# Two attention heads in one transpose of the output, and three pieces of work moved by up to one unit

## The reference

```python
z = jnp.einsum("bsd,dc->bsc", rms_norm(x, norm_mix_g), w_in)      # columns B | C | h | q | k | v, 512 each
y_conv = B * (conv3(C * h) + conv_b)                              # causal, width 3, by channel
q, k = rms_norm(q, q_gain), rms_norm(k, k_gain)                   # 8 heads of 64
scores = jnp.einsum("bnqhd,bnkhd->bhnqk", q, k_band) * 64 ** -0.5 + bias   # chunks of 64, this and 8 before
o = jnp.einsum("bnhqk,bnkhd->bnqhd", softmax(scores), v_band)
x = x + concat(group_rms_norm(y_conv), group_rms_norm(o)) @ w_out # groups of 64
out = x + square(relu(rms_norm(x, norm_mlp_g) @ w_mlp_in)) @ w_mlp_out
```

## Time and profile before

| | us |
|---|---|
| median of 3 runs | 1124.91 |
| lowest, highest | 1124.46, 1125.86 |
| the profiled execution | 1123.81 |
| its span, first to last instruction | 1122.0 |
| PE busy in it | 1100.3 |
| DVE, ACT, POOL busy in it | 714.0, 538.9, 629.2 |

### The profile page before, as it was taken

The page is one execution under the profiler, slowest core; times in us unless marked ns, Lnnn a source line. Parts: engine busy times, 40 slices in busy tenths (PEclk is TensorE's granted clock), DMA queues, the critical chain, the costliest instruction groups (busy, mean ns, idle before and its releaser), DMA issues.

```text
span 1122.0 us, 14684 instructions
## 1 busy us (share of the span) xinstructions
PE 1100.3 (98%) x5272; PEld 918.0 (82%) x5272; DVE 714.0 (64%) x899; ACT 538.9 (48%) x885; POOL 629.2 (56%) x368
## 2 busy tenths in 40 slices
PE   5999999999999999999999999999999999999998
PEld 5888888888888878887888888888878888888887
DVE  6677757767766785335435353534477767777798
ACT  6664665465476563225454545445453243333330
POOL 4322141230412030267778888787789697796992
PEclk9999999999999999999999999999999999999999
DMA  8311110120110514121464444444687435345324
GB/s 254 107 38 38 41 56 16 40 58 19 56 29 31 188 58 150 57 75 62 155 197 151 153 150 149 150 146 163 236 287 244 155 122 188 129 134 204 113 76 168
DMA packets 98511, 135.79 MB, mean 121 GB/s; under 512 B 8072, under 2 KB 52112, under 8 KB 98456
## 3 DMA queue, kind: packets, MB, share of 16 engines
q1 hardware_dynamic: 95104, 131.13, 34.9%
q10 hardware_dynamic: 3352, 3.94, 1.2%
HBM read 97.27 MB, written 39.34 MB: 122 GB/s over the span
## 4 chain that ended last, share of the span: by engine, by line
PE 93%; POOL 2%; DVE 2%; DMA 1%; ACT 1%; issue 1%; ACTq 0%; SPq 0%; POOLq 0%; DVEq 0%
PE PJ L1530 22%; PE PJ L1785 10%; PE SC L1785 9%; PE OS L1785 7%; PE PJ L1608 7%; PE PJ L1822 7%; PE SC L1822 7%; PE PT L1822 6%; PE OS L1822 6%; PE OS L1590 3%; PE PT L1577 2%; PE SC L1567 1%; PE SC L1566 1%; PE SC L1608 1%; DMA b<-in_w_mlp_out 1%
## 5 line engine op out<-in xcount | busy, mean ns | idle before, releaser
L1530 PE MATMUL PJ<-actT,wsl 128*128 128x512 f32 (+1 forms) x1176 | 298.2, 396 | 1.0 <-DVE actT L1012 0.9
L1530 PEld LDWEIGHTS PJ<-actT,wsl 128*128 128x128 f32 x1176 | 209.7, 190 | 38.9 <-DVE actT L1012 1.7
L614 POOL TENSOR_TENSOR ring<-b,ring 128x1024 fp32r<-128x1024 f32 x48 | 139.0, 2905 | 34.9 <-ACT ring L957 34.6
L1434 DVE TENSOR_TENSOR ring<-hraw,ring 128x1024 fp32r<-128x1024 f32 x56 | 148.8, 2693 | 3.5 <-ACT ring L952 3.5
L505 POOL CAST wsl<-raw 128x1024 fp32r<-128x1024 f32 x24 | 26.0, 1082 | 197.3 <-PE PJ L1530 164.5
L952 ACT ACTIVATE ring<-hraw 128x1024 fp32r<-128x1024 f32 x56 | 59.2, 1057 | 131.3 <-PE OS L1822 60.1
L1785 PE MATMUL OS<-actT,w1a 128*128 128x512 f32 x384 | 93.6, 391 | 0.8 <-ACT p1s L893 0.8
L731 ACT ACTIVATE prob<-prob,negm 128x640 f32<-128x640 f32 (+4 forms) x64 | 44.4, 694 | 90.8 <-DVE negm L1117 90.6
L1785 PEld LDWEIGHTS OS<-actT,w1a 128*128 128x128 f32 x384 | 71.6, 188 | 15.6 <-issue 1.2
L1822 PE MATMUL PJ<-ring 128*128 128x512 f32 x336 | 80.6, 390 | 2.1 <-POOL ring L614 2.1
L1822 PE MATMUL PT<-ring 128*128 128x512 f32 x336 | 80.8, 390 | 0.1
(11 more groups left out here) (195 smaller groups left out, 2189.0 us busy)
## 6 DMA issues: line engine op xcount, KB each, us to landing
hraw<-hidd SPq DMA_DIRECT2D x56, 512.0 KB, 3.7
w1r<-in_w_mlp_in SPq DMA_DIRECT2D x16, 1024.0 KB, 6.3
hidd<-hs SPq DMA_DIRECT2D x64, 256.0 KB, 2.0
b<-in_w_mlp_out SPq DMA_DIRECT2D x16, 1024.0 KB, 7.0
raw<-in_w_in SPq DMA_DIRECT2D x24, 512.0 KB, 3.8
hidd<-h SPq DMA_DIRECT2D x48, 256.0 KB, 2.3
xin<-in_x SPq DMA_DIRECT2D x8, 512.0 KB, 8.6
woraw<-in_w_out SPq DMA_DIRECT2D x8, 512.0 KB, 9.0
```

What stands on the lines that cost most here:

```text
L614: nc.gpsimd.tensor_tensor(duo(n)[1][LO], W2_SRC[name][:, 2 * d:2 * d + 2], duo(n)[1][HI].bitcast(F32), ALU.subtract).then_inc(s["wl2_done" ...
L1434: vec.tensor_tensor(duo(n)[0][LO], hraw[:, n % HRING], duo(n)[0][HI].bitcast(F32), ALU.subtract).then_inc(s["hl2_done"], 1)
L1530: last = mm(PJ[:, g % 2, cols], wsl[:, w % NSLOT, a, k], actT[:, b, k, c], start=(r == 0), stop=(r == 3 * KD - 1))
```

## The change

**Two heads in one transpose.** `u_sum` now makes two instructions. A reduce on the lower 64 partitions of UP adds the two halves of columns there (V's HI), into the half of `uT` that belongs to the unit's head. Then an add takes UP's upper 64 partitions (V's LO), of which only the columns of `pT` HI are read, onto it; the product LO*LO, which was summed before, falls away. It waits for the reduce by a new semaphore, `fold_done`. So `uT` holds two heads, 64 partitions each, and `pair_transpose` runs once for two units, in the heads of the odd units from 3 on and once behind unit 15. `o_sum` becomes a copy of 128 columns. `prob_v(u)` waits for `us_done` of the unit before, as no transpose ahead of it does so any longer.

**Moves.** DVE: V's remainder `v_lo(it, 1)` from 7a to 6b, `inverse(4, 0)` from 11a to 11b. PE: `sum_squares(4)` from 10b to 11a; `sum_squares(it+1, 1)` behind 22 projections from the last `prob_v` on, and not 18; the number of projections of the turn stays 54. ACT: `deviation(4)` from unit 10 to unit 11. In the last pass `pair_transpose(7)` stands behind `sum_squares(5)` and six products of `w_out`, as `u_transpose(15)` did. No DMA is changed.

The diff:

```diff
--- before.py
+++ after.py
@@ -212,7 +212,7 @@
         p1s_done r11_done u2_done u4_done c12_done c21_done c22_done
         rl11_done rl12_done rl21_done rl22_done h11_done h12_done h21_done h22_done hs_done
         b11_in b12_in b21_in b22_in hh2_done wh2_done hl2_done wl2_done ts_done d2_done dr_done
-        acc_in acc_zero fin_done
+        acc_in fold_done fin_done
         """.split()
         s = {n: ctx.enter_context(nc.semaphore(n)) for n in names}
         PRIMED = 3
@@ -795,6 +795,7 @@
                     if u == 10:
                         o_dev(it, 0)
                         c_copy(it, 1)
+                    if u == 11:
                         deviation(it, 4)
                     if u == 12:
                         o_store(it, 0)
@@ -1127,18 +1128,19 @@
             def u_sum(it, u):
 
                 dve.wait_ge(s["pv_done"], it * UNITS + (u + 1))
-                if u >= 2:
-                    dve.wait_ge(s["uq_done"], it * UNITS + (u - 1))
-                vec.tensor_reduce(uT[:, u % 2], UP.rearrange("p b c -> p c b"), AX.X, ALU.add
-                                  ).then_inc(s["us_done"], 1)
+                j, rows = u // 2, HEADS[u % 2]
+                if j >= 2 and u % 2 == 0:
+                    dve.wait_ge(s["uq_done"], it * (UNITS // 2) + j - 1)
+                vec.tensor_reduce(uT[rows, j % 2], UP[0:HD].rearrange("p b c -> p c b"), AX.X, ALU.add).then_inc(s["fold_done"], 1)
+                dve.wait_ge(s["fold_done"], it * UNITS + (u + 1))
+                vec.tensor_tensor(uT[rows, j % 2], UP[HD:P, 0], uT[rows, j % 2], ALU.add).then_inc(s["us_done"], 1)
 
             og = on[:, :, :].rearrange("p g (u d) -> p g u d", d=HD)
 
             def o_sum(it, j):
 
-                dve.wait_ge(s["uq_done"], it * UNITS + 2 * (j + 1))
-                vec.tensor_reduce(og[:, j // 4, 2 * (j % 4):2 * (j % 4) + 2], UQ.rearrange("p (u a d) -> p u d a", u=2, a=2),
-                                  AX.X, ALU.add).then_inc(s["oq_done"], 1)
+                dve.wait_ge(s["uq_done"], it * (UNITS // 2) + j + 1)
+                vec.tensor_copy(on[:, j // 4, j % 4 * P:(j % 4 + 1) * P], UQ[:, j % 2 * P:(j % 2 + 1) * P]).then_inc(s["oq_done"], 1)
 
             def per_unit(a):
                 return a[:, :].rearrange("p (u o) -> p u o", o=1).broadcast_to([P, 8, HD])
@@ -1198,8 +1200,9 @@
                     qk_lo(it, 2)
                 if at == "6a":
                     qk_lo(it, 3)
+                if at == "6b":
+                    v_lo(it, 1)
                 if at == "7a":
-                    v_lo(it, 1)
                     conv_gate(it, 0)
                 if at == "7b":
                     conv_tap(it, 0, 0)
@@ -1214,6 +1217,7 @@
                     squares_lo(it, 4)
                 if at == "11a":
                     o_norm(it, 0)
+                if at == "11b":
                     inverse(it, 4, 0)
                 if at == "12a":
                     inverse(it, 4, 1)
@@ -1584,6 +1588,8 @@
                 pe.wait_ge(s["ptlo_done"], it * UNITS + (u + 1))
                 if u == 0:
                     pe.wait_ge(s["vlo_done"], it * 2 + 1)
+                if u:
+                    pe.wait_ge(s["us_done"], it * UNITS + u)
                 if u % 2 == 0 and u:
                     pe.wait_ge(s["oq_done"], it * (UNITS // 2) + u // 2)
                 for j in range(nb):
@@ -1592,9 +1598,9 @@
                               start=(j == 0), stop=(j == nb - 1))
                 last.then_inc(s["pv_done"], 1)
 
-            def u_transpose(it, u):
-                pe.wait_ge(s["us_done"], it * UNITS + (u + 1))
-                nc.tensor.transpose(UQ[:, u % 2 * P:(u % 2 + 1) * P], uT[:, u % 2], ident[:, :]).then_inc(s["uq_done"], 1)
+            def pair_transpose(it, j):
+                pe.wait_ge(s["us_done"], it * UNITS + 2 * (j + 1))
+                nc.tensor.transpose(UQ[:, j % 2 * P:(j % 2 + 1) * P], uT[:, j % 2], ident[:, :]).then_inc(s["uq_done"], 1)
 
             def o_transpose(it, g, turn):
                 pe.wait_ge(s["on_done"], it * 2 + (g + 1))
@@ -1645,7 +1651,7 @@
                         sum_squares(it, 3)
                     if at == "4b":
                         v_transpose(it, 1)
-                    if at == "10b":
+                    if at == "11a":
                         sum_squares(it, 4)
                     if at == "12a":
                         o_transpose(it, 0, OTURN[0])
@@ -1664,8 +1670,8 @@
                 fill(4)
                 for u in range(UNITS):
                     count = (FILL_LAST if last else FILL)[u] - (4 if u == 0 else 0)
-                    if u >= 2:
-                        u_transpose(it, u - 2)
+                    if u >= 3 and u % 2:
+                        pair_transpose(it, u // 2 - 1)
                     if u + 1 < UNITS:
                         score(it, u + 1)
                     fill(count // 2)
@@ -1679,23 +1685,21 @@
 
                     rest = REST + 4 * 3 * KD - n
                     fill(rest - 54)
-                    u_transpose(it, UNITS - 2)
                     prob_v(it, UNITS - 1)
                     fill(8)
-                    u_transpose(it, UNITS - 1)
-                    fill(10)
+                    pair_transpose(it, UNITS // 2 - 1)
+                    fill(14)
                     sum_squares(it + 1, 1)
-                    fill(18)
+                    fill(14)
                     v_transpose(it + 1, 0)
                     fill(18)
                     o_transpose(it, 1, OTURN[1])
                 else:
                     assert n == REST
-                    u_transpose(it, UNITS - 2)
                     prob_v(it, UNITS - 1)
                     sum_squares(it, 5)
                     w_out_both(1, (1,))
-                    u_transpose(it, UNITS - 1)
+                    pair_transpose(it, UNITS // 2 - 1)
                     for k in range(2, KD):
                         w_out_both(k)
                         if k == 4:
```

## The result

The changed kernel takes 1130.11 us (median of 10 runs, 1127.19 to 1132.35), beside 1125.22 for the kernel before on the same chip (10 runs, 1124.25 to 1126.52). The ratio is 1.0046, 95% interval 1.0038 to 1.0055: slower by 4.9 us, where 2.6 us less was predicted. The profiled execution took 1129.81 us, its span 1128.0 (before 1122.0).

What follows compares the result with a forecast made beforehand. PE, busy 98% of the span, was taken as the bound. Passes 0 to 2 gave -2.39, the turns -0.6, the last pass +0.35: -2.6 us off 1124.91, so 1122.3 us, range 1120.2 to 1126.0.

Steps and rivals of the forecast that it cites:

- The wait for `sql` at the turn: Between passes, PE's 0.59 us wait for POOL goes or falls under 0.1; about 0.2 net gained, -0.6 over three turns.
- The first minimum: At the turn, PE's score(1) must wait for unit 0's minimum from DVE; 0.15 to 0.24 of the 0.59 stays.
- The two instructions of the fold: u_sum on DVE becomes a reduce of 0.42 and an add of 0.29; the next instruction starts 0.43 later.
- The two taps of unit 13: Passes 0 to 2: DVE taps alternate with POOL, end where they did; one of 8 transposes gives nothing, leaving -0.80 per pass.
- the last pass is late at `pT` and at `ym_lo(0)`: Last pass: PE waits longer for unit 13's pT and gets ym_lo(0) about 1.0 us later.
- Rival A: At the turn POOL takes the port first, kL's second subtract waits, 1.1 later three times: 1125.6 us; chance 0.25.
- Rival C: The add across halves costs twice the nearest row or more, u_sum +0.9; several units wait: 1128.8 us; chance 0.10.
- the transposes: On PE in the four passes, 32 fewer at 0.114 us each: -3.65 us if PE stays the limit.
- step 1: In unit 6, the pT remainder's 1.13 us spare shrinks to 0.16, the closest of the ordinary units, still without a wait.
- step 2: Last pass: ym_lo(0) about 1.0 us later, against five transposes and the tail's: +0.35 us instead of -0.91.

Runs made afterwards that it cites:

- e4: Changed kernel with q's remainder of the second half, qk_lo(2), made on DVE behind unit 4 instead of unit 5: 1127.07 us, ratio 1.0016.
- e1: Kernel before with the fold and pair transposes alone, all moves undone: 1133.02 us, ratio 1.0073.
- e2: Kernel before with the moves alone, one transpose a head as before: 1124.82 us, ratio 1.0005.
- e3: Changed kernel with sum of squares 4 and its root back at their old places in the last pass only: 1129.66 us, ratio 1.0032.
- e8: Kernel before with two unread DVE products added ahead of unit 13's taps in the last pass: 1128.66 us, ratio 1.0029.
- e6: Changed kernel with the score of unit 15 computed three times instead of once in the last pass: 1128.60 us, ratio 1.0020.
- e12: e11 with o_sum(6) ahead of ym_lo(1) on DVE in the last pass: 1122.60 us, ratio 0.9982.
- e7: e5 with the repeated score of e6 added: 1124.92 us, ratio 0.9992.
- e10: Kernel before with one unread DVE product added at 13a in the last pass: 1125.36 us, ratio 1.0010.
- e5: Changed kernel with the edits of e3 and e4 together: 1125.43 us, ratio 0.9997.
- e11: e5 with a tap at 12b outside the last pass, ym_lo(0), o_sum(6) and pair transpose 6 reordered in it, and e6's repeated score: 1124.19 us, ratio 0.9993.

## Why the prediction was wrong

**Right.** The wait for `sql` at the turn went: from `prob_v(15)` to V's transpose it is 9.6 us for 10.1, where 0.59 was forecast. The first minimum took a part back, as forecast: PE is 0.16, 0.07 and 0.32 later behind `score(1)` of passes 1 to 3, for 0.15 to 0.24. The two instructions of the fold cost 0.42 + 0.29. The two taps of unit 13 still end where POOL lets them, and `prob_v(13)` waits 0.25 instead of 0.15, so the one transpose fewer ahead of it gives nothing; the last pass is late at `pT` and at `ym_lo(0)`. Rival A did not happen: the second `kL` row in the turn stayed at its length. Rival C did not either, as the add costs no more than its nearest row; that its 1128.8 is near the result is luck. Passes without the new wait (e4: 93.8) are 0.6 shorter than before's, where the forecast had 1.0; 0.17 of the difference is e4's own new wait at `prob_v(4)`. No run left out the transposes alone; pass 0 of the changed kernel prices them at 0.13 to 0.14 each.

**Wrong, step 1: "That is the closest of the ordinary units; 0.16 remain."** I asked for each unit when its `pT` remainder was ready, and not for the other things that a score waits for. `score(8)` also reads `kL` of the half of k made just before, and had about 0.2 to spare with two sums ahead of it. e1 has the wait with the fold alone, e2 has none without the fold, and e4 takes it away. A pass was to take 93.45 us and took 94.49 in the mean. For the sum: the span grew by 6.0 us, of which 4.0 are half clock, so 2.0 is left where -2.6 was forecast. Of the 4.6 between them, 3.2 arose in passes 0 to 2 (+0.17 for -3.0), which is three of these waits at 1.1 each. In the last pass the products of `w_out` start 2.16 later, where the forecast's term gave 0.43 (1.0 less five transposes): 1.7 more, of which 1.0 is the fourth wait and 0.5 stands under step 2. The changed kernel's pass 0 begins 0.3 earlier, ahead of anything that was changed.

**Wrong, step 2: the last pass as "+0.35", at full clock.** The lateness in this term was too small: from `score(15)` to the products of `w_out` it is 5.90 us (396.94 to 402.84), before 4.43 (396.38 to 400.81), so 1.47 more, where I had 1.0. e3, with the root at its old place, has 0.96 more, so the moved root has 0.5 of it, for which I had 0.26. Its price was wrong altogether: I took every duration of PE from a profile at 1.00 and did not ask whether longer pauses would change that. In the profile after, pauses of 1.8 + 0.7 + 0.8 us stand in 5.4 us (397.4 to 402.8; before 0.8 + 0.3 + 0.8). Behind the second the clock falls to half for 6.8 us, and 2.4 us are lost by the rows; 1.6 more go in the second stretch. e8 makes the loss without the change, e6 makes it rarer by adding work, and in e12's profile it is gone.

The Trainium skill, "TensorE: Matmul & The Clock Gate", Part 1 (The HAM clock gate), says that the gate goes back to half rate when PE has been idle, and warns of an idle gap longer than any pause in front of a first stretch here. On the two levels the trace agrees (six products in 1.66 or in 2.93 us). On the gap it does not: the longest of those pauses was 2.0 us (e8), and in e7 the clock fell behind pauses of 0.1, 0.7 and 0.9. In front of the second stretch stands one longer pause, of 2.1 us in after and 3.9 in e4.

**What stays open.** The second stretch, 834.8 to 838.2 in the profile after, stands at PE's wait for POOL's `ring`, a wait that every kernel here has. After, and e4:

```profile
834.43 4.58 PE L1826 MATMUL PJ<-ring 128*128 128x512 f32 x12 [2.11 <-POOL ring L614]
```

```profile
832.20 4.50 PE L1826 MATMUL PJ<-ring 128*128 128x512 f32 x12 [3.92 <-POOL ring L614]
```

It is 2.1 us before and 2.4 in e12, where no stretch follows in the profile. In these profiles a second stretch came only where a first had come, but not in e10. One profile for each kernel can't tell what connects them, and 1.6 us hang on it. Why the wait is 3.1 to 3.9 us in e3, e4 and e5 was not traced either. Of the three pauses in the last pass the first counts: filled, it took the runs at 0.995 or below from eight of ten to none (after, e6) and from four of eleven to none (e5, e7). No run changed the second by itself. e12 shortened the last one of e11 from 1.4 to 0.5, and neither has a run below 0.997.

## What to carry to other kernels

When an instruction becomes longer on an engine in the middle of a chain, list for every consumer all the semaphores it waits for, not the one that came last in the trace before: the second latest had 0.2 us to spare, and the change used 0.86. Look at PE's pauses together with their neighbours, and price the products behind them at both clock levels; a pause can be worth filling with work that is thrown away. And look at the clock of every run before a median of few runs is believed: here the same kernel has runs that are 4 us apart by it.
